# Triangular inversion on stacked 64-column diagonal blocks in a hybrid encoder layer

## What is computed

```python
lc = min(t_, CHUNK)                       # CHUNK = 64
gcum = jnp.cumsum(gc, axis=-1)
decay = jnp.exp(jnp.where(tril, gcum[..., :, None] - gcum[..., None, :], -jnp.inf))
kb = kc * bc[..., None]
a = jnp.where(strict, jnp.einsum('nbhid,nbhjd->nbhij', kb, kc) * decay, 0.0)
ia = a + jnp.eye(lc, dtype=jnp.float32)
u = lax.linalg.triangular_solve(ia, vc * bc[..., None], left_side=True, lower=True, unit_diagonal=True)
w = lax.linalg.triangular_solve(ia, kb * jnp.exp(gcum)[..., None], ...)
...
v_new = u_i - jnp.einsum('bhld,bhdv->bhlv', w_i, s)
o_i = einsum(q_i * exp(g_i), s) + einsum(qk_i, v_new)
s = s * jnp.exp(g_last)[..., None] + jnp.einsum('bhld,bhlv->bhdv', k_i * jnp.exp(g_last - g_i)[..., None], v_new)
```

## Time and profile before

| | |
|---|---|
| median of three runs | 1982.66 us |
| the profiled execution | 1982.78 us |
| its span, first to last instruction | 1981.2 us |
| mean granted TensorE clock | 0.995 |
| GDN heads in the loop, each | 54.0 us |

### The profile page before, as it was taken

How to read it: one execution, slowest core, us unless ns; L and a number is a source line. 1 busy time by engine, 2 the same in 40 slices (tenths; PEclk the granted TensorE clock), 3 DMA queues, 4 the chain that set the end, 5 groups by cost and what they waited for, 6 DMA issues and landing times.

```text
span 1981.2 us, 31761 instructions
## 1 busy us (share of the span) xinstructions
PE 1929.6 (97%) x9924; PEld 1620.5 (82%) x9924; DVE 1033.1 (52%) x2226; ACT 742.7 (37%) x1504; POOL 168.0 (8%) x268
## 2 busy tenths in 40 slices
PE   7999999999999999999999999999999999999996
PEld 7999998787777787878888888888888888888884
DVE  7555656666667675464444444433334444343446
ACT  4444444444444442343333333333333333333331
POOL 1111111222112220000111110000000000000000
PEclk9999999999999999999999999999999999999998
DMA  7555554433333333434444444344344444444342
GB/s 224 152 141 153 142 154 112 104 97 89 85 103 96 108 104 118 144 97 124 144 126 136 132 130 126 124 130 129 127 128 123 133 124 125 127 127 167 125 129 89
DMA packets 241440, 249.94 MB, mean 126 GB/s; under 512 B 26488, under 2 KB 159616, under 8 KB 240736
## 3 DMA queue, kind: packets, MB, share of 16 engines
q1 hardware_dynamic: 234192, 233.60, 41.0%
q0 software_dynamic: 7184, 15.52, 2.6%
HBM read 237.67 MB, written 11.35 MB: 126 GB/s over the span
## 4 chain that ended last, share of the span: by engine, by line
PE 90%; DVE 6%; issue 2%; ACT 1%; DMA 0%; DVEq 0%; POOL 0%; SPq 0%; POOLq 0%; ACTq 0%
PE bank L258 72%; PE bank L1548 6%; PE bank L278 2%; DVE w_lo L243 1%; DVE work_a L1270 1%; PE bank L1099 1%; PE bank L1659 1%; PE bank L1093 1%; PE bank L1081 1%; PE bank L1075 1%; PE bank L363 1%; PE bank L1149 0%; DMA x_res<-in_x_sample 0%; PE bank L1112 0%; PE bank L547 0%
## 5 line engine op out<-in xcount | busy, mean ns | idle before, releaser
L243 DVE TENSOR_TENSOR w_lo<-raw,w_hi 128x512 fp32r<-128x512 f32 (+2 forms) x848 | 577.5, 689 | 699.2 <-ACT w_hi L238 694.0
L238 ACT ACTIVATE w_hi<-raw 128x512 fp32r<-128x512 f32 (+2 forms) x848 | 516.5, 617 | 825.1 <-PE bank L258 727.5
L258 PE MATMUL bank<-w_hi,aT_hi 128*128 128x512 f32 (+2 forms) x1824 | 720.3, 395 | 8.7 <-ACT gbuf L910 3.9
L258 PE MATMUL bank<-w_hi,aT_lo 128*128 128x512 f32 (+2 forms) x1824 | 692.6, 380 | 0.0
L258 PE MATMUL bank<-w_lo,aT_hi 128*128 128x512 f32 (+2 forms) x1824 | 690.8, 379 | 0.0
L258 PEld LDWEIGHTS bank<-w_hi,aT_hi 128*128 128x128 f32 x1824 | 343.5, 188 | 71.6 <-issue 15.3
L258 PEld LDWEIGHTS bank<-w_hi,aT_lo 128*128 128x128 f32 x1824 | 342.6, 188 | 58.1
L258 PEld LDWEIGHTS bank<-w_lo,aT_hi 128*128 128x128 f32 x1824 | 344.1, 189 | 47.7
L258 PE MATMUL bank<-w_hi,hT_hi 128*128 128x512 f32 x468 | 183.2, 391 | 0.4 <-DVE x_res L1724 0.3
L258 PE MATMUL bank<-w_hi,hT_lo 128*128 128x512 f32 x468 | 182.2, 389 | 0.0
L258 PE MATMUL bank<-w_lo,hT_hi 128*128 128x512 f32 x468 | 182.2, 389 | 0.0
(11 more groups left out here) (329 smaller groups left out, 1743.7 us busy)
## 6 DMA issues: line engine op xcount, KB each, us to landing
raw<-in_ffn_w_gate SPq DMA_DIRECT2D x176, 256.0 KB, 2.7
raw<-in_ffn_w_up SPq DMA_DIRECT2D x176, 256.0 KB, 2.7
raw<-in_ffn_w_down SPq DMA_DIRECT2D x176, 256.0 KB, 3.0
raw<-in_w_in SPq DMA_DIRECT2D x128, 192.0 KB, 2.4
raw<-in_w_in SPq DMA_DIRECT2D x128, 128.0 KB, 2.2
raw<-in_w_in SPq DMA_DIRECT2D x256, 64.0 KB, 2.2
raw<-in_w_out SPq DMA_DIRECT2D x61, 256.0 KB, 3.0
work_b<-in_cache_fox_k POOLq DMA_DIRECT2D x8, 512.0 KB, 4.5
```

Of the source, the lines that this page charges most:

```text
L238: nc.scalar.activation(w_hi[:, g % RING, 0:width], raw[:, g % RAW, 0:width], ACT.Copy).then_inc(sem("w_high"), 1)
L243: nc.vector.tensor_tensor(w_lo[:, g % RING, 0:width], raw[:, g % RAW, 0:width], w_hi[:, g % RING, 0:width], ALU.subtract).then_inc(sem("w_ ...
L258: last = nc.tensor.matmul(acc[t][:, 0:width], l[:, k0 + n, t * P:(t + 1) * P], r[:, g % RING, 0:width], start=(n == 0 and j == 0), stop=(n ...
```

## The change

- T, U and Z hold only the two 64x64 blocks on the diagonal of each 128x128 matrix, one above the other: 64 columns in place of 128. For levels 1 to 5 the products are made as two 64x64 matmuls, one in the upper left corner of the array (rows 0 to 63), one in the lower right (rows 64 to 127). `times` and `turn` write these two. The transposes of these levels are matmuls with the identity.
- Level 6 is one 64x64 block. It is made from four small instructions, and a full matrix `UF` takes the two diagonal blocks and this one for the products v0 and v1.
- `passed()` puts a semaphore increment of TensorE behind the waits and ahead of the small matmuls.
- The levels' slots move from 18, 23, 26, 29, 32, 34 to 18, 21, 24, 28, 31, 34. Two of the three last steps of the convolution of part 2 move from ahead of level 1 to behind it (`conv`); `silu(2)`, the norm and `nv` move to later levels; v2 moves to slot 36, the first of the streams to slot 40, v1 to 41, the other streams and the outputs to 42; VectorE's chain on `go` is due at 42 and its state updates at slot 45.
- ScalarE's eight decays of S move behind level 6.
- In the output projection the first matmuls of the second column block wait on three finer events in place of `g_o` and `g_state`.
- The constants shrink (six masks of 64 columns in place of seven of 128).

The diff, cut to its core:

```diff
-LEVEL_AT = (0, 18, 23, 26, 29, 32, 34)
+LEVEL_AT = (0, 18, 21, 24, 28, 31, 34)
...
-                T = sb(ctx, "g_T", [P, TT, P])
+                T = sb(ctx, "g_T", [P, TT, HALF])
...
+                    def turn(bk, at, x, t):
+                        for b in two:
+                            ins = nc.tensor.matmul(tl(bk, at, HALF)[b], x[b, t, :], ident[b, b], start=True, stop=True)
+                        return ins
+                    def times(bk, at, l, r, t):
+                        for b in two:
+                            ins = nc.tensor.matmul(tl(bk, at, HALF)[b], l(b, t), r[b, t, :], start=True, stop=True)
+                        return ins
...
-                    nc.tensor.transpose(tl(b7, 0), T[:, 0, :], ident).then_inc(sem("g_U1a_ps"), 1)
+                    passed()
+                    turn(b7, 0, T, 0).then_inc(sem("g_U1a_ps"), 1)
...
+                        passed()
+                        if last_level:
+                            nc.tensor.matmul(tl(b4, 0, HALF)[upper], A[lower, 0, upper], U[lower, 0, :], start=True, stop=True)\
+                                .then_inc(sem("g_Za_ps"), 1)
+                            nc.tensor.transpose(tl(b5, 1, HALF)[upper], U[upper, 0, :], ident[upper, upper])\
+                                .then_inc(sem("g_Ta_ps"), 1)
...
+                        else:
+                            times(b4, 0, of_A, U, 0).then_inc(sem("g_Za_ps"), 1)
+                            if n > 1:
+                                turn(b5, 1, U, 0).then_inc(sem("g_Ta_ps"), 1)
...
-                        if n == 3:
+                        if n == 5:
                             W("g_nv")
...
+                    yield LEVELS_DONE - 1
+                    W("g_qkdT")
+                    passed()
+                    for b in two:
+                        last = nc.tensor.matmul(tl(b3, 0)[b], U[b, 2, :], R[b, 2, :], start=True, stop=True)
+                    last.then_inc(sem("g_v2_ps"), 1)
...
+                    yield LEVELS_DONE + 3
                     W("g_vm")
-                    streams(0), streams(1)
+                    streams(0).then_inc(sem("g_St_ps"), 1)
+                    yield LEVELS_DONE + 4
+                    L("g_Ub", LEVELS, LEVELS), W("g_R1")
+                    nc.tensor.matmul(tl(b6, 0), UF[:, 1, :], R[:, 1, :], start=True, stop=True)\
+                        .then_inc(sem("g_v1_ps"), 1)
+                    yield LEVELS_DONE + 5
+                    streams(1)
...
-                    conv(2, range(TAP - 1))
+                    conv(2, range(1))
...
                         if n == 1:
+                            conv(2, range(1, TAP - 1))
+                        if n == 2:
                             silu(2)
...
-                    yield LEVELS_DONE + 4
+                    yield LEVELS_DONE + 5
                     W("g_o_ps"), W("g_oq2")
...
                     ins.then_inc(sem("g_o"), 1)
-
+                    yield LEVELS_DONE + 8
                     W("g_S2_ps"), W("g_S1")
...
                             elif t == 0:
-                                pe.wait_ge(sem("g_o"), HEADS)
+                                pe.wait_ge(sem("g_own"), G_OWN * (HEADS - 1) + G_READ)
+                            elif t == 1:
+                                pe.wait_ge(sem("g_S1_new"), HEADS)
                             else:
                                 pe.wait_ge(sem("g_state"), HEADS + 1)
```

More of the change, by code:

```diff
@@ L87 @@
 G_OWN = 32
+G_READ = 22
 STORE_AT = 12
@@ L112, in constants @@
     c[:, C_MS + P:C_MS + 2 * P] = np.where((col <= row) & same, 0, NEG)
[L113 removed]
+    col = row // HALF * HALF + i[None, :HALF]
+    for n in range(LEVELS - 1):
         s = 1 << n
[L115 to L116 removed]
+        r, k = (row, col) if n == 0 else (col, row)
+        c[:, C_LV + n * HALF:C_LV + (n + 1) * HALF] = (r // (2 * s) == k // (2 * s)) & (r // s % 2 == 1) & (k // s % 2 == 0)
+    c[:, C_IC:C_IC + HALF] = row == col
     c[:, C_BM:C_BM + NB] = row // NQ == np.arange(NB)[None, :]
@@ L1015, in encoder_layer @@
                 cvb = (b4, b5, b3)
-                lv = [cn[:, C_LV + n * P:C_LV + (n + 1) * P] for n in range(LEVELS)]
+                lv = [cn[:, C_LV + n * HALF:C_LV + (n + 1) * HALF] for n in range(LEVELS - 1)]
+                unit = cn[:, C_IC:C_IC + HALF]
+                two = (slice(0, HALF), slice(HALF, P))
+                upper, lower = two
                 def n_tiles(level):
@@ L1072, in gdn_pe @@
                             last.then_inc(sem("g_qk_ps"), 1)
-                        if n == 5:
+                        if n == 6:
                             W("g_qkd")
[L1075 to L1083, removed]
-                            for t in range(1, n_tiles(n)):
-                                last = nc.tensor.transpose(b7[:, (t - 1) * P:t * P], U[:, t, :], ident)
-                            last.then_inc(sem("g_Tb_ps"), 1)
+                        last_level = n == LEVELS - 1
@@ new lines, in gdn_pe @@
+                        passed()
[4 more added lines that the diff above has]
+                                .then_inc(sem("g_Ta_ps"), 1)
+                            L("g_Ub", n, LEVELS)
+                            passed()
+                            nc.tensor.matmul(tl(b6, 1, HALF)[upper], A[lower, 1, upper], U[lower, 1, :], start=True, stop=True)\
+                                .then_inc(sem("g_Zb_ps"), 1)
+                            nc.tensor.transpose(tl(b7, 0, HALF)[upper], U[upper, 1, :], ident[upper, upper])\
+                                .then_inc(sem("g_Tb_ps"), 1)
+                        else:
+                            times(b4, 0, of_A, U, 0).then_inc(sem("g_Za_ps"), 1)
+                            if n > 1:
+                                turn(b5, 1, U, 0).then_inc(sem("g_Ta_ps"), 1)
+                            L("g_Ub", n, LEVELS)
+                            passed()
+                            for t in range(1, n_tiles(n)):
+                                last = times(b6, t, of_A, U, t)
+                            last.then_inc(sem("g_Zb_ps"), 1)
+                            if n > 1:
+                                for t in range(1, n_tiles(n)):
+                                    last = turn(b7, t - 1, U, t)
+                                last.then_inc(sem("g_Tb_ps"), 1)
@@ L1097, in gdn_pe @@
                             L("g_Tb", n - 1, LEVELS - 2)
[L1098 to L1101, removed]
+                        passed()
+                        if last_level:
+                            nc.tensor.matmul(tl(b7, 2, HALF)[upper], T[upper, 1, :], Z[upper, 1, :], start=True, stop=True)\
+                                .then_inc(sem("g_UZb_ps"), 1)
+                        else:
+                            for t in range(1, n_tiles(n)):
+                                last = times(b7, t + 1, of_T, Z, t)
+                            last.then_inc(sem("g_UZb_ps"), 1)
+                        if n == 3:
                             L("g_cv", 3, 3)
@@ L1236, in gdn_act @@
                     nc.scalar.activation(S1[:], b4[:, 0:P], ACT.Copy).then_inc(sem("g_S1"), 1)
+                    decays(range(2, 5))
+                    yield LEVELS_DONE + 4
+                    decays(range(5, NB)).then_inc(sem("g_Sdec"), 1)
                     yield 48
```

134 lines of the change are left out of this document (83 added, 51 removed).

## The result

The changed kernel takes 1991.32 us (median of 6, 1989.75 to 1991.43) against 1982.50 beside it: a ratio of 1.0039, 95% interval 1.0029 to 1.0050. It is slower by 8.8 us, where 4.0 were forecast on the earlier median. Four of the six executions lie at 1991.2 to 1991.4 and two, the profiled among them, at 1989.8; why wasn't found. The profiled execution took 1989.75 us with a span of 1988.2, 7.0 us over the span before.

The account below looks back on a forecast made before the run. TensorE, busy 97% of the span, was taken as the bound. Own work +16.9, waits going -16.5, waits coming +3.1 and +0.4 gave +3.9 on 1982.8: 1986.7 us, range 1974 to 2005.

Parts of the forecast that it names:

- the lone stream: Parting the streams adds one more visit to a tiled shape, 0.84 us a head.
- TensorE's own work: Visits 4.8 plus parted stream 0.84 less 3.55 saved on small products: +2.1 us a head, +16.9 for eight.
- Rival 2: Inversion's 64-column rounds take more than half of 0.11; at 0.08 each 17 us slower, 2003; chance 0.15.
- A visit at 0.36: Entering and leaving the 64x64 shape costs 0.36 us, between 0.33 and 0.42 of existing shapes; 14 visits a head.
- Rounds of 0.055: Inversion's 64-column rounds, both corners side by side, take 0.055 us, half of a 128-column record's 0.11.
- Rival 3: The two corners run one after another, a round costs 0.11: 37 us more, 2024; chance 0.07.
- Rival 4: passed() increments, 27 a head, keep TensorE from loading weights ahead: 17 us more, 2004; chance 0.08.
- Waits that go: TensorE's waits at level 1, level 5, v1 and from head to head go or shrink, together 16.5 us.
- head to head: TensorE's wait between one head and the next, 0.92 us seven times, goes: 6.4 us.
- Waits that come: New wait of 0.45 us at the last transposes, 3.1 in all, and 0.4 more in the output projection.
- ScalarE's decays at nothing: Moving ScalarE's decays and copies costs nothing, as ScalarE has 29 us of idle time a head.
- Rival 1: Faster: waits at level 1 and last transposes don't come (6.7), a visit costs 0.33 (3.1): 1976.9; chance 0.20.

Follow-up runs that it names:

- E3: Changed kernel with level 6's two transposes made as products with the identity in the same corner: 1986.65 us, ratio 1.0016 to the kernel before.
- E11: Changed kernel with level 6's first part reordered, both products and then both transposes: 1989.34 us, ratio 1.0031 to the kernel before.
- E2: Changed kernel with streams(0) and streams(1) together again behind v1: 1990.66 us, ratio 1.0036 to the kernel before.
- E5: Changed kernel with the first two streams paired again and ScalarE's six later state decays three slots later: 1983.93 us, ratio 1.0001 to the kernel before.
- E1: Changed kernel's whole order of work with the inversion's old 128x128 products and turns: 1982.94 us, ratio 0.9994 to the kernel before.
- E4: Changed kernel with ScalarE's second group of squares one slot later: 1986.68 us, ratio 1.0014 to the kernel before.
- E10: Changed kernel, 64x64 corners, level 6's turns as products, waits repaired, first decays ahead of qkdT's copy, v2 in v0's slot: 1975.30 us, ratio 0.9960 to before.
- E9: New order, old 128x128 forms, five repairs, first decays ahead of qkdT's copy, v2 in v0's slot: 1968.87 us, ratio 0.9926 to the kernel before.
- E6: Kernel before with only VectorE's state updates moved to slot 45: 1978.94 us, ratio 0.9978.

## Why the prediction was right, and where its sizes were off

The direction and the mechanism were right: visits and the lone stream against waits, nearly one for one. The forecast was +3.9 for the profiled execution, which shows +7.0; the median adds the rest, since it lies 1.6 us over that execution.

- **TensorE's own work**: forecast 2.1 us a head, measured 2.52 (the table's blocks, waits apart), 3.3 us more over eight. All of it is one term. Level 6 was to be level, 0.72 for two visits less 0.66 for its work; it costs 0.48 more than before (0.40 in its first part, 0.08 in its second). Its first part was to take 0.22 besides the visit. That was right for products alone: E3 has it (0.57 less 0.36). I took the transposes of a corner to run like that too, beside the products and without a price, as line 1078 stands among full products at none. In the change six records run one after another, 0.35 for 0.22, and E3 and E11 show 0.09 to 0.13 us for each of three switches. (Rival 2 counts six rounds for level 6, where this sum has eight; that changes nothing in the result.)
- **A visit at 0.36**: right. Level 2's second part has six rounds, 0.35 us, and costs 0.69; level 4's four rounds, 0.23, and 0.58. That is 0.34 and 0.35. At level 5, where the 128x32 products follow at once, it was 0.16 (0.15). The lone stream cost 0.83 (0.84).
- **Rounds of 0.055**: 0.058, so rival 2 falls. Rival 3 falls by the pairs 6 ns apart. Rival 4 falls too: the first pairs are 0.107 us apart, but that is within the 0.34 of a visit, and the pair behind a block's second increment comes in step (669.65, 0.059 behind the one before).
- **Waits that go** (forecasts in brackets), forecast 16.5, measured 15.4: level 1 0.67 a head and 0.2 at the end, 4.9 (5.1); level 5 0.28, 2.2 (2.2); v1 0.23, 1.8 (2.8); head to head 0.92, 6.5 (6.4). At v1 0.11 stayed (0.34 against 0.23 without a wait); E2 and E5 show that with the pair it is the decays that make R1 late.
- **Waits that come**, forecast 3.5, measured 3.2: last transposes 0.32 seven times, 2.3 (3.1), the output projection 0.2 (0.4), and the final block's 0.08, not forecast, 0.7.
- **ScalarE's decays at nothing**: the number held by luck, the reason didn't. I took 29 us of idle time a head as cover. The place counts: three decays ahead of a split are 1 us on the chain split, split, R1, v1. Only the lone stream, which I booked as pure cost, kept that out of the result. The 0.17 at v2 and 0.22 at the outputs in E1 look like the same thing, copies behind splits that decays hold up, but no run took them apart.

By these terms 20.2 - 15.4 + 3.2 = +8.0 in the stage; start-up and the rest differ by about -1.

Rival 1, the faster case, failed on its waits: both came, at 0.55 and 0.32. E4 shows that a one-line edit would have removed the first.

## What to carry to other kernels

Count visits, not columns: here a visit to a tiled shape cost 0.35 us and one product in corners saved 0.11, so three products a visit don't pay (0.33 for 0.35) and two less so; E10 against E9 shows it with most waits gone. Try order and shape apart before you judge a change that has both: one moved block alone (E6) gained 4.6 us, and the mended order with the old forms gained 14, where the whole change lost 9. And an idle engine's work is free only at places where nothing stands behind it; two faults can hide each other, so take away a cost and look at what becomes late.

## What the runs showed of the hardware that was not expected

- In a 64x64 corner each switch between matmul and transpose costs 0.09 to 0.13 us (with the visit's 0.36 taken off the block is 0.71 with three inner switches and 0.44 with one, and six records of 0.058 are 0.35 of either; the difference of the two is 0.13 a switch). Between full 128x128 forms none is seen: in the kernel before, level 3's first part, three products and three transposes, takes 0.994 us, nine records of 0.11.
- Two 64-row tiles onto the same 64 columns, writing different banks, start within 10 ns of each other (E3). So do two corners that write the same bank at other partitions (669.370 and 669.377 in the changed kernel).
- One more semaphore wait ahead of the last streams goes with 0.09 us, though in the changed kernel the stream that it waits for had started over 3 us earlier. It came and went together with other edits only, so the wait as its cause isn't shown.
